# First norm and first four output tiles of a two-block transformer, taken feature tile by feature tile

## What is computed

```python
def rmsnorm(x, g):
    xf = x.astype(jnp.float32)
    y = xf * lax.rsqrt(jnp.mean(xf * xf, axis=-1, keepdims=True) + EPS)
    return (y * g.astype(jnp.float32)).astype(x.dtype)

def modulate(x, shift, scale):
    return x * (1 + scale) + shift

def swiglu(u, w_in, w_out):
    a, b = jnp.split(u @ w_in, 2, axis=-1)
    return (jax.nn.silu(a) * b) @ w_out

    cond = jax.nn.silu(c)
    ...
        mod = cond @ w_ada[l] + b_ada[l]
        sh1, sc1, gt1, sh2, sc2, gt2, sh3, sc3, gt3 = [
            m[:, None, :] for m in jnp.split(mod, N_MOD, axis=-1)]
        u = modulate(rmsnorm(h, g_norm_ffn1[l]), sh1, sc1)
        h = h + 0.5 * gt1 * swiglu(u, w_ffn1_in[l], w_ffn1_out[l])
```

## Time and profile before

| | us |
|---|---|
| median of the runs shown | 2701.93 |
| the profiled execution's own time | 2698.95 |
| span from its first to its last instruction | 2697.1 |
| busy: TensorE (matmul), VectorE, ScalarE | 2531.8, 1851.8, 1101.2 |
| first matmul of tile 0 | 43.35 |
| first matmul of 13d | 87.02 |

### The profile page before, as it was taken

The page is one execution under the profiler, slowest core; times in us unless marked ns, Lnnn a source line. Parts: engine busy times, 40 slices in busy tenths (PEclk is TensorE's granted clock), DMA queues, the critical chain, the costliest instruction groups (busy, mean ns, idle before and its releaser), DMA issues.

```text
span 2697.1 us, 39723 instructions
## 1 busy us (share of the span) xinstructions
PE 2531.8 (94%) x15724; PEld 2282.1 (85%) x15724; DVE 1851.8 (69%) x3539; ACT 1101.2 (41%) x1631; POOL 0.2 (0%) x4
## 2 busy tenths in 40 slices
PE   4999989889989999899999899999899999798997
PEld 4998889789988888688888898888898888777997
DVE  7878977788879965535555569886584444575665
ACT  3444555344453323634222652222642222545443
POOL 0000000000000000000000000000000000000000
PEclk8999999989989999999999999999999999898999
DMA  8876846768767742422222266665273332312552
GB/s 310 299 247 201 269 160 232 263 228 288 246 197 251 221 138 68 146 94 86 86 91 90 86 189 206 191 196 195 87 269 122 94 101 76 92 57 74 186 185 96
DMA packets 161097, 452.65 MB, mean 168 GB/s; under 512 B 17680, under 2 KB 21264, under 8 KB 160912
## 3 DMA queue, kind: packets, MB, share of 16 engines
q1 hardware_dynamic: 160912, 450.11, 51.2%
HBM read 448.99 MB, written 1.05 MB: 167 GB/s over the span
## 4 chain that ended last, share of the span: by engine, by line
PE 58%; DVE 6%; ACT 4%; issue 1%; DMA 0%; SPq 0%; ACTq 0%; DVEq 0%
PE PS L985 18%; PE PS L986 18%; PE PS L987 18%; DVE wlo L1445 2%; ACT whi L1189 1%; PE PS L1006 1%; PE PS L1008 1%; DVE X L1534 1%; PE PS L1124 1%; DVE X L1532 1%; ACT NT L1242 1%; DVE RS L1501 1%; PE PS L1170 0%; DVE Ul L1538 0%; PE PS L1153 0%
## 5 line engine op out<-in xcount | busy, mean ns | idle before, releaser
L1445 DVE TENSOR_TENSOR wlo<-raw,whi 128x1024 fp32r<-128x1024 f32 x602 | 736.1, 1223 | 490.3 <-ACT whi L1189 487.6
L985 PE MATMUL PS<-Uh,wlo 128*128 128x256 f32 (+1 forms) x2992 | 972.8, 325 | 77.4 <-DVE Ul L1538 42.0
L986 PE MATMUL PS<-Ul,whi 128*128 128x256 f32 (+1 forms) x2992 | 954.3, 319 | 0.0
L987 PE MATMUL PS<-Uh,whi 128*128 128x256 f32 (+1 forms) x2992 | 954.2, 319 | 0.0
L1189 ACT ACTIVATE whi<-raw 128x1024 fp32r<-128x1024 f32 x602 | 632.7, 1055 | 718.7 <-PE PS L987 716.9
L985 PEld LDWEIGHTS PS<-Uh,wlo 128*128 128x128 f32 x2992 | 580.9, 194 | 131.3 <-issue 44.9
L986 PEld LDWEIGHTS PS<-Ul,whi 128*128 128x128 f32 x2992 | 583.5, 195 | 35.0 <-issue 0.2
L987 PEld LDWEIGHTS PS<-Uh,whi 128*128 128x128 f32 x2992 | 582.6, 195 | 34.9
L985 PE MATMUL PS<-Hh,wlo 128*128 128x256 f32 (+1 forms) x1616 | 529.5, 328 | 9.9 <-DVE X L1428 4.1
L986 PE MATMUL PS<-Hl,whi 128*128 128x256 f32 (+1 forms) x1616 | 514.1, 318 | 0.0
L987 PE MATMUL PS<-Hh,whi 128*128 128x256 f32 (+1 forms) x1616 | 513.9, 318 | 0.0
(11 more groups left out here) (170 smaller groups left out, 1918.9 us busy)
## 6 DMA issues: line engine op xcount, KB each, us to landing
MODS<-in_mm SPq DMA_DIRECT2D x168, 256.0 KB, 3.7
SCR<-in_mm SPq DMA_DIRECT2D x168, 256.0 KB, 3.7
raw<-in_f0i SPq DMA_DIRECT2D x64, 512.0 KB, 3.8
raw<-in_f1i SPq DMA_DIRECT2D x56, 512.0 KB, 3.5
raw<-in_f2i SPq DMA_DIRECT2D x56, 512.0 KB, 3.6
SCR<-in_ma SPq DMA_DIRECT2D x88, 256.0 KB, 5.0
raw<-in_w1i SPq DMA_DIRECT2D x44, 512.0 KB, 4.4
raw<-in_w2i SPq DMA_DIRECT2D x44, 512.0 KB, 4.3
```

The costliest lines, as they stand in the source:

```text
L985: e.matmul(o, ll, rh, start=start, stop=False)
L986: e.matmul(o, lh, rl, start=False, stop=False)
L987: return e.matmul(o, lh, rh, start=False, stop=stop)
L1445: e.tensor_tensor(wlo[:, w.n % RING, :], raw[:, w.n % RING, :], whi[:, w.n % RING, :].bitcast(F32), ALU.subtract).then_inc(s["wlo"].tell(w ...
```

## The change

The scale and the shift of the first norm are computed by feature tile: the 32 mods are put in another order (`mod_tile`), so that mods 0 to 15 give feature tiles 0 to 3 of both vectors, and mods 16 to 31 the other four, four mods for each. Half 1 of a feature tile now comes directly behind half 0. X is loaded after the first eight mod loads. The coefficient of the norm is made for feature tiles 0 to 3 at once, then one by one. The first four output tiles are no longer multiplied one after the other: `first_stage` takes four banks, and for each feature tile k TensorE makes the three passes of all four tiles (`by_feature`). The four splits of these tiles stand behind the first four feature tiles of the norm; the next four splits (chunks 4 to 7) stand behind the last products. `ffn` begins with the third pair (`early=2`), and the rate of mods is lowered after 8 more chunks, at the same place of the plan as before.

```diff
+def mod_tile(m):
+    if m < 32:
+        return m % 4 // 2, m % 2, m // 4
+    return m // 16, m % 16 // 8, m % 8
...
+def first_stage(p):
+    tiles = [(what, f) for f in SLABS[0] for what in ("gate", "up")]
...
+    banks = tuple(p.bank() for _ in tiles)
...
+    for _ in range(16):
+        p.mod_step()
+    t = p.tallied(LAT, 1e-6, (0, 0))
+    coefs(0, 4)
+    for k in range(4):
+        norm(k, 0)
+    norm(4, 2)
+    for _ in tiles:
+        p.split_next()
+    for k in range(4):
+        products(k)
+    for _ in range(4):
+        p.mod_step()
+    for k in range(4, KT):
+        coefs(k, k + 1)
+        norm(k, 1)
+        if k < KT - 1:
+            p.mod_step()
+        norm(k + 1, 2)
+        products(k)
+        if k < KT - 1:
+            for _ in range(3):
+                p.mod_step()
+    p.norming = False
+    for i, (what, f) in enumerate(tiles):
+        p.split_next()
+        j = p.pairs
+        p.put(what, st="w1i", n=i, r=LAT, bank=banks[i], f=f, j=j, after=("first", i))
+        p.used[i] = ("first", i)
...
-    while p.mod_fetch(0) and p.mod_loads < 16:
-        pass
+    while p.mod_loads < 8:
+        p.mod_fetch(0)
     p.put("xload")
+    while p.mod_loads < 16:
+        p.mod_fetch(0)
     for _ in range(RING):
         p.fetch()
...
-    p.rms("n1", 0, 0, "g1", (0, 0), None, ahead=LEAD)
+    first_stage(p)
     for who in (1, 2):
         p.put("condload", q=who, n=who)
         p.put("cond", q=who, n=who)
     p.rate = 1.4
-    main = p.ffn("w1", "w1o", LAT, [(("w1", 0), "half", 0, 2)], False)
+    main = p.ffn("w1", "w1o", LAT, [(("w1", 0), "half", 0, 2)], False, early=2)
     p.put("ctxload")
-    for _ in range(12):
+    for _ in range(8):
         next(main)
     p.rate = 0.72
     p.put("maskload")
...
+                elif w.what == "by_feature":
+                    for i, b in enumerate(w.banks):
+                        on.wait_ge(s["wlo"], i)
+                        on.wait_ge(s["ulo"], ("n1", w.k))
+                        m = three(PS[:, b[0], lo:hi], *weights(i, w.k), Uh[:, w.k, lo:hi], Ul[:, w.k, lo:hi],
+                                  w.k == 0, w.k == KT - 1)
+                        if w.k == KT - 1:
+                            m.then_inc(s["matmul"].tell(("first", i)), 1)
```

More of the change, by code:

```diff
@@ L86, in piece_of, with mod_number, mod_key @@
     return min(i for i, o in enumerate(SECTIONS) if o == (group, sec, half) or o == (group, sec, 2))
-def mod_key(which, sec):
+def mod_tile(m):
+    if m < 32:
+        return m % 4 // 2, m % 2, m // 4
+    return m // 16, m % 16 // 8, m % 8
+def mod_number(p, half, j):
+    return 4 * j + 2 * p + half if p < 2 else 16 * p + 8 * half + j
+def mod_key(which, sec, j=7):
     p = piece_of(which, sec)
-    return (16 * p + 15, [w for _, w in PIECES[p][2]].index(which))
+    return (mod_number(p, 1, j if p < 2 else 7), [w for _, w in PIECES[p][2]].index(which))
 def mod_slot(m):
@@ L231, in mod_until @@
     def mod_until(self, which, sec):
-        while self.mods < 16 * (piece_of(which, sec) + 1):
+        while self.mods < 16 * max(piece_of(which, sec) + 1, 2):
             self.mod_step()
@@ L469, in through, with coefs, norm, products @@
         return w
+def first_stage(p):
+    tiles = [(what, f) for f in SLABS[0] for what in ("gate", "up")]
+    for what, f in tiles:
+        p.stream.append(("w1i", f if what == "gate" else FT + f))
+    at = len(p.coefs)
+    banks = tuple(p.bank() for _ in tiles)
+    def coefs(a, b):
+        p.coefs["n1", "c", b - 1] = at
+        p.put("coef", st="g1", at=at, f=1, k=a, n=b, after=("n1", "c", b - 1))
+    def norm(k, part):
+        p.put("rms", st="n1", k=k, n=t["n"], r=LAT, at=part, gates=(("n1", "c", max(k, 3)),))
+    def products(k):
+        p.put("by_feature", st="w1", k=k, r=LAT, banks=banks)
+    for _ in range(16):
[27 more added lines that the diff above has]
+        p.used[i] = ("first", i)
+        if what == "up":
+            p.pairs += 1
+            p.hidden("w1", f, slots_of(SLABS)[f], j, LAT)
+def product_key(w):
+    return w.after or (w.id, 0)
 def schedule(total):
@@ L936, in sync @@
                     if 16 <= m < 32:
[L937 removed]
+                        on.wait_ge(s["modded"], (m - 16, len(PIECES[mod_tile(m - 16)[0]][2]) - 1))
                     elif m >= 36:
@@ L941, in sync @@
                         on.wait_ge(s["matmul"], last_mix)
-                    name, sec, _, _ = PIECES[m // 16]
-                    e.dma_start(MB[mod_slot(m)], T[name][sec, m % 16]).then_inc(s_mod[mod_slot(m)], 16)
+                    piece, half, j = mod_tile(m)
+                    name, sec, _, _ = PIECES[piece]
+                    e.dma_start(MB[mod_slot(m)], T[name][sec, 8 * half + j]).then_inc(s_mod[mod_slot(m)], 16)
                 elif w.what == "xload":
@@ L1009, in tensor @@
                              stop=w.final, skip_group_check=True).then_inc(s["matmul"].tell(("sums", w.j)), 1)
+                elif w.what == "by_feature":
[6 more added lines that the diff above has]
+                            m.then_inc(s["matmul"].tell(("first", i)), 1)
+                elif w.what in ("gate", "up") and w.after:
+                    pass
                 elif w.what in ("gate", "up", "pool_in", "qk1", "sigmoid", "gu", "qk2"):
@@ L1211, in scalar @@
                     e.activation(RS[:, h, 0, :], RS[:, h, 0, :], ACT.Sqrt).then_inc(s["std"].tell(w.n), 1)
-                elif w.what == "rms" and w.k < KT:
+                elif w.what == "rms" and w.k < KT and w.at != 2:
                     on.wait_ge(s["normed"], (w.st, w.k))
-                    on.wait_ge(s["modded"], mod_key(w.q, w.f))
+                    on.wait_ge(s["modded"], mod_key(w.q, w.f, w.k))
                     if w.after:
@@ L1260, in scalar @@
                 elif w.what == "gate":
-                    on.wait_ge(s["matmul"], (w.id, 0))
+                    on.wait_ge(s["matmul"], product_key(w))
                     if w.j >= 2:
@@ L1447, in vector @@
                 elif w.what == "mod":
-                    name, sec, whose, bias = PIECES[w.n // 16]
-                    half, j = w.n % 16 // 8, w.n % 8
+                    piece, half, j = mod_tile(w.n)
+                    name, sec, whose, bias = PIECES[piece]
                     slot = mod_slot(w.n)
@@ L1480, in vector @@
                     else:
-                        on.wait_ge(s["modded"], mod_key(w.q, w.f))
-                        e.scalar_tensor_tensor(out=o, in0=mod(w.q, w.f), scalar=1.0, in1=vecs(kind), op0=ALU.add,
-                                               op1=ALU.mult).then_inc(s["coef"].tell(key), 1)
+                        c = slice(w.k, w.n or KT)
+                        on.wait_ge(s["modded"], mod_key(w.q, w.f, c.stop - 1))
+                        e.scalar_tensor_tensor(out=o[:, c], in0=mod(w.q, w.f)[:, c], scalar=1.0, in1=vecs(kind)[:, c],
+                                               op0=ALU.add, op1=ALU.mult).then_inc(s["coef"].tell(key), 1)
                 elif w.what == "stat":
```

11 lines of the change are left out of this document (6 added, 5 removed).

## The result

The changed kernel takes 2714.94 us, the median of four runs (2714.05 to 2716.97); beside it the kernel before took 2701.78. The ratio is 1.0051, with a 95% interval of 1.0038 to 1.0064: 13.2 us slower. The forecast was 2711.0, 9.1 slower: the sign and the chain of causes were right, and the loss was sized too small. The measured time lies above 2713.4, the upper bound to which the forecast's own terms add up. The profiled execution of after is the longest of the four, with a span of 2715.2 us.

A forecast was written before the change was run, and what follows sets the result against it. Before 49 us the norm's chain on VectorE was taken to bound the kernel, behind it TensorE. 6.9 us late at 13d plus 2.2 of slow clock gave 9.1 us slower, 2711.0 us; range 2699 to 2715.

The forecast's parts named there:

- the conditions: Two condition loads, queued in SyncE's list behind four fetches, land at 62.7 and 64.0; ScalarE waits, tile 8 starts at 68.3.
- the burst: Five mods left for right ahead of 12a's coefficient; their late loads make them take 7.2 us in place of 3.4.
- The new start: Start of the stage: reordered mods and earlier X let TensorE start at 29.7, 13.7 us earlier than before.
- The rival that the reordering would not bring TensorE forward: Mods wait for loads behind X, first matmul later than 33, total over 2715; chance 0.08 together with other losses.
- Feature tiles 4 to 7: VectorE's norm chain sets the end, 3.8 us per feature tile; tile 4 starts at 52.5 instead of 58.94, 6.4 won.
- the pair wait: On VectorE, half 1 of a mod waits for half 0 right ahead of it: 0.12 us each.
- VectorE's chain to the burst: After standing idle from 58.7 to 67.1, VectorE works without a stop on splits, mods and products until 84.8.
- The sum at 13d: 13d, the first matmul needing an accumulate of VectorE, starts at 93.9 instead of 87.02: 6.9 us late, bounds +2.9 to +8.4.
- The clock: TensorE's clock is slow after standing still 8 us ahead of 13d, costing 1.3 to 3.1 us; 2.2 taken.
- (1): Rival: condition loads land before ScalarE finishes split 7, so their wait is hidden; 13d at 88.2, total 2705.2; chance 0.14.
- (2): Rival: as (1), and the five mod loads are there in time; 13d at 84.3, total 2699.2; chance 0.10.
- (3): Rival: VectorE and the loads have unseen slack and all 6.4 us won at tile 4 stay; total 2695.5; chance 0.06.

The follow-up runs named there:

- halves apart: Changed kernel with each group of four mods reordered: half 0 of scale, half 0 of shift, then both halves 1; 2712.71 us, ratio 1.0038.
- the other two with its start: Kernel before with no mods in its first four chunks, so five come at once: 2710.96 us; kernel before with the context load behind the twelve chunks: 2701.56 us.
- conditions early: Changed kernel with the two condition loads issued right behind the norm, their Silus left in place; 2706.95 us, ratio 1.0021.
- all moved: Changed kernel with condition loads right behind the norm, four mods in VectorE's idle time, rate 1.5, context and masks loaded later; 2697.64 us, ratio 0.9987.
- both, context later: Changed kernel with condition loads right behind the norm, mod rate 2.0 instead of 1.4, and the context load behind the eight chunks; 2698.8 us, ratio 0.9992.
- the best kernel: The changed kernel with the edits of all moved and the mod order of halves apart; 2695.11 us, ratio 0.998 against the kernel before.

## Why the prediction was right in kind and short in size

The step that failed is how long a queued load takes to land: the sum let loads follow each other at the pace of a lone or an early load, so that the conditions came 1.8 us later, and the burst took 2.0 us longer, than it said. Its second mis-sized term is the wait between the two halves of a mod, 0.12 us where 0.22 was measured, which made 1.2 us of tile 4. The causes and their order held.

**The new start: right.** First product 30.90, net of the load's start (1.01) 29.9, forecast 29.7. The rival that the reordering would not bring TensorE forward is out.

**Feature tiles 4 to 7: 1.2 short.** Tile 4 was forecast for 52.5 and started at 54.74, net 53.7. The term is the pair wait: 0.12, taken from a coefficient that waited for a mod, where a mod that waits for a mod loses 0.22 to 0.23, and once 0.64. The mods 16 to 19 took 3.56 instead of 2.9, a feature tile 3.91 instead of 3.8. The run with the halves apart shows the whole term, the part that was in the sum too: 2.4 us at tile 4.

**The conditions: right in kind, 1.8 short.** SyncE issued them at 60.33 (net 59.3; 58.0 was forecast, with the 1.2 from ahead), ScalarE stood at their Silu, VectorE idled, TensorE had a hole ahead of tile 8; all four were named. But the second landed at 68.18, net 67.2, not 64.0, and `wlo` 8 began at net 70.1, not 67.1: 3.0 late, 1.2 of it from ahead. The sum let a queued 512 KB follow the load ahead of it by 1.3 us; the third fetch landed at 64.16, 3.35 us behind the second (60.81).

**VectorE's chain to the burst: right.** From `wlo` 8 to the fifth mod from the end it was forecast as 67.1 to 84.8, 17.7 us; it took 71.11 to 88.81, 17.7 us.

**The burst: right in kind, 2.0 short.** It took 9.38 instead of 92.2 - 84.8 = 7.4. Mod 45 was to land 3.6 behind its issue; it was issued at 87.57 and landed at 93.45, 5.88 later, because the fetch ahead of it landed 2.85 behind its predecessor. That is the same mistake as with the conditions: a landing time of a lone load used in a stretch whose load queue is 0.95 busy. The trace of before had the better number: its own fetches from 56 to 66 us took 5.8 us to land (median of four), not 3.6 (DMA view):

```profile
raw<-in_w1i SPq DMA_DIRECT2D x4, 512.0 KB, 5.8
```

**The sum at 13d.** 1.2 + 1.8 + 2.0 = 5.0 too little; net 92.46 - 80.55 = 11.9, where 6.9 was forecast, with an upper bound of 8.4. The bound let one chain be 1.5 longer, and all three terms were off in the same direction. (The lower bound has a slip: 93.9 less the 3.8 that the loads cost is 90.1, not 89.9.)

**The clock: right in kind, 0.6 short.** Granted was 0.50 in all of the window from 99.90 to 106.00, 6.1 us of work, and the 198 matmuls from 13d on took 2.8 us longer than in before; 2.2 was forecast, in a range of 1.3 to 3.1. The medians can't tell this term: there 13.2 - 11.9 = 1.3 us are left behind 13d, and over the table that difference goes from -0.4 to 3.5. The terms together are 5.0 + 0.6 = 5.6 short, the medians' difference only 13.2 - 9.1 = 4.1; some 1.0 of the rest may be what before's own trace won at tile 4 over the other two with its start.

**The rivals.** (1), hidden conditions, is what the run with the conditions early makes true by hand: it forecast 13d at 88.2 and 2705.2, and measured was 91.24 (net of the first mod's later start 90.8) and 2706.95, with a wait of 2.44 us left in the burst. (2) and (3) needed VectorE and the loads to have slack. They have some: with all moved TensorE never waits from tile 4 on, at 330 GB/s and a share of 0.94, VectorE busy for 16.94 of 18 us. So the forecast that VectorE is "behind for good" holds for this order of steps alone. Its idle 10.18 us were the loss, not a lack of its time. The Trainium skill's warning under (2), "TensorE: Matmul & The Clock Gate", "HAM oscillation", came true in the row: with groups of 12 matmuls between waits the granted clock was 1.00 at 46 to 48 and 0.50 at 50.7 to 54.0. It cost little, as VectorE's chain set the pace there: by an estimate from two groups 0.4 us, where rival (2) had an estimated 2. The three matmuls that finish tile 0, and that the split of chunk 4 waits for, took 1.01 us from 51.27 on; the first three at k = 5, from 43.45 on, took 0.62. The page's drain behind a table load ("ScalarE: Activation LUTs", "What ACT_TABLE_LOAD costs", 1.38 us) is absent here too: the load at 53.45 took 1.28, and the Silu started at 54.74.

**What stays open.** Why queued loads land so late from 56 us on. In part the loads had gaps: from 57.5 to 59.0 they move only 85 GB/s, as the second fetch was issued at 57.36 and the third at 58.83. But from 60.81 to 64.16, while the third was awaited, they moved 1.03 MB (307 GB/s, share 0.95), twice the 512 KB that landed, so loads issued behind it were moved along with it; from 89.94 to 92.79, ahead of mod 45, it was 0.82 MB for 512 KB. Up to 46 us, at 378 to 397 GB/s and shares of 1.04 to 1.07 in before, a 512 KB load landed 1.3 us behind the one ahead. The context's load isn't the cause: with it moved away (both, context later) the third fetch still landed 2.71 behind the second. A busy TensorE alone isn't it either: from 34 to 44 us the loads move 339 GB/s at a share of 0.88 with TensorE busy for 8.66 of 10 us, from 62 to 68 it is 337 at 0.98. No run takes it apart. Nor is it shown where the best kernel loses 1.7 of its 7.5 us behind 13d; its first 198 matmuls there took 23.86 us for 23.76, so it is not the clock right behind 13d.

## What to carry to other kernels

An earlier start is worth what the next wait leaves of it: follow every queue that the moved steps pass, and list for each load between the old and the new place who waits for it. Here a head start of 5 us turned into a loss of 13 by the place of two kinds of loads in one in-order list (conditions and masks) and by a budget of mods counted in chunks, of which there were now fewer, and a third load (the context) was next in line; put right, the same start gives 3.4 us, and 5.8 with the halves apart. And size a queued load by the landings of the busiest stretch that the trace shows, not by a lone one.

## What was not expected of the hardware

- A mod that reads the sum of the mod right before it starts 0.22 us later than an independent one; one mod between them hides it, worth 2.4 us at tile 4 here.
- A 512 KB load landed 1.3 us behind the one ahead of it up to 46 us, but up to 3.35 us behind it later, at 0.95 of the load engines' time instead of 1.04 to 1.07; in those 3.35 us twice its bytes were moved.
- The first mod starts at 6.34 to 7.87 us, another time in each execution, and the whole first stage with it. In ten of the twelve traces it waits for its own load, in two for ScalarE's Silu of the condition. Milestones of two traces are compared net of it.
- 198 matmuls behind 13d took 23.8 us with no hole ahead of them, and 25.3 to 26.6 with one of 2.8 to 9.4 us.
